# Where the transposed X of a blocked triangular inverse comes from: TensorE's transposes, or VectorE's 32x32 blocks

## The reference, cut to what matters

```python
def wkv_scan(r, decay, k, v, a_vec, b_vec, s0, reverse):
    def step(s, inp):
        r_t, w_t, k_t, v_t, a_t, b_t = inp
        sa = jnp.einsum('bhvk,bhk->bhv', s, a_t)
        s = s * w_t[:, :, None, :] + sa[..., None] * b_t[:, :, None, :] + v_t[..., None] * k_t[:, :, None, :]
        return s, jnp.einsum('bhvk,bhk->bhv', s, r_t)
```

## Time and profile before

| | us |
|---|---|
| median of 3 runs | 3042.59 (3038.54 to 3043.01) |
| profiled execution, own time | 3039.05 |
| profiled execution, span | 3036.8 |
| recurrence, first to last start of `begin_x` (15 steps) | 383.1 |
| PE busy over the whole span | 2760.7 (91%) |
| DVE, ACT, POOL busy over the whole span | 1139.7, 945.8, 177.7 |

### The profile page before, as it was taken

How to read it: one execution, slowest core, us unless ns; L and a number is a source line. 1 busy time by engine, 2 the same in 40 slices (tenths; PEclk the granted TensorE clock), 3 DMA queues, 4 the chain that set the end, 5 groups by cost and what they waited for, 6 DMA issues and landing times.

```text
span 3036.8 us, 57743 instructions
## 1 busy us (share of the span) xinstructions
PE 2760.7 (91%) x25062; PEld 1841.5 (61%) x25062; DVE 1139.7 (38%) x1685; ACT 945.8 (31%) x1575; POOL 177.7 (6%) x231
## 2 busy tenths in 40 slices
PE   8999999999998999999999989899999988866665
PEld 6877777878777878865333332346788774423332
DVE  4545555545455565442000011423545534000001
ACT  4435454434445555432010001103334321100000
POOL 0002000000002000000000000002223210000000
PEclk9999999999999999999999999999999999978778
DMA  6474245575663355534999999711000027999998
GB/s 252 178 284 158 98 142 184 188 276 192 232 226 111 125 193 201 181 119 185 408 421 421 421 421 420 316 68 63 10 16 10 10 76 305 380 421 421 418 421 343
DMA packets 101400, 707.11 MB, mean 233 GB/s; under 512 B 11780, under 2 KB 12548, under 8 KB 18224
## 3 DMA queue, kind: packets, MB, share of 16 engines
q1 hardware_dynamic: 90864, 657.17, 55.1%
q10 hardware_dynamic: 9648, 43.91, 3.7%
q0 software_dynamic: 656, 2.52, 0.2%
HBM read 702.47 MB, written 1.07 MB: 232 GB/s over the span
## 4 chain that ended last, share of the span: by engine, by line
PE 67%; DMA 19%; DVE 6%; ACT 5%; issue 2%; SPq 0%; POOL 0%; ACTq 0%; DVEq 0%; POOLq 0%
DMA weight_ring<-in_stream 19%; PE banks L2040 8%; PE banks L650 7%; PE banks L652 7%; PE banks L651 7%; PE banks L1870 3%; PE banks L2405 3%; PE banks L1017 3%; PE banks L1019 2%; PE banks L1018 2%; PE banks L2451 2%; ACT front L1281 1%; PE banks L1177 1%; PE banks L2826 1%; PE banks L2836 1%
## 5 line engine op out<-in xcount | busy, mean ns | idle before, releaser
L2040 PE MATMUL banks<-weight_ring,scratch 128*32 128x256 f32 (+1 forms) x4304 | 560.1, 500 | 153.4 <-DMA weight_ring<-in_stream 151.8
L2040 PEld LDWEIGHTS banks<-weight_ring,scratch 128*32 128x32 f32 (+1 forms) x4304 | 184.1, 128 | 510.5 <-DMA weight_ring<-in_stream 261.6
L647 DVE TENSOR_TENSOR split_high<-weight_ring,split_high 128x1024 fp32r<-128x1024 f32 x198 | 242.1, 1229 | 258.9 <-ACT split_high L642 258.3
L642 ACT CAST split_high<-weight_ring 128x1024 fp32r<-128x1024 f32 x198 | 206.8, 1052 | 288.9 <-PE banks L652 223.1
L2191 DVE TENSOR_TENSOR scratch<-scratch,banks 128x512 f32<-128x512 f32 (+1 forms) x32 | 17.7, 554 | 573.0 <-PE banks L2040 573.0
L1369 DVE TENSOR_TENSOR split_high<-weight_ring,split_high 128x1024 fp32r<-128x1024 f32 x128 | 161.6, 1273 | 160.4 <-ACT split_high L1266 160.4
L650 PE MATMUL banks<-split_high,features_low 128*128 128x512 f32 x480 | 189.8, 395 | 0.0
L652 PE MATMUL banks<-split_high,features_high 128*128 128x512 f32 x480 | 187.1, 390 | 0.0
L651 PE MATMUL banks<-split_high,features_high 128*128 128x512 f32 x480 | 186.8, 389 | 0.0
L1266 ACT CAST split_high<-weight_ring 128x1024 fp32r<-128x1024 f32 x128 | 133.4, 1049 | 165.3 <-PE banks L1019 159.3
L1017 PE MATMUL banks<-split_high,features_low 128*128 128x512 f32 x392 | 158.6, 405 | 11.2 <-DVE split_high L1369 7.6
(11 more groups left out here) (423 smaller groups left out, 4673.4 us busy)
## 6 DMA issues: line engine op xcount, KB each, us to landing
weight_ring<-in_stream SPq DMA_DIRECT2D x624, 1024.0 KB, 10.7
scratch<-in_kept ACTq DMA_DIRECT2D x20, 1024.0 KB, 10.3
scratch<-in_pair_rows ACTq DMA_DIRECT2D x8, 448.0 KB, 3.6
scratch<-in_kept ACTq DMA_DIRECT2D x6, 512.0 KB, 6.5
scratch<-in_lora ACTq DMA_DIRECT2D x2, 1536.0 KB, 17.8
front<-in_gain_rows ACTq DMA_DIRECT2D x5, 512.0 KB, 3.7
bias<-bias_rows POOLq DMA_DIRECT2D x1, 2304.0 KB, 15.6
scratch<-in_routing ACTq DMA_DIRECT2D x1, 1040.5 KB, 4.9
```

The source lines that it names most:

```text
L642: act.copy(split[i % 4][0], source(i)).then_inc(*self.rounded.up())
L647: dve.tensor_tensor(lo, source(i), hi.bitcast(F32), ALU.subtract).then_inc(*self.rest.up())
L2040: last = pe.matmul(self.psum[q * M:(q + 1) * M, (GATE, UP, DOWN)[part], 0:W], left, w[j][:, q * W:(q + 1) * W], start=(k == 0), stop=(k == ...
```

## The change

The four transposes behind each `z` and ACT's copy into XT go. In their place stands `turn_x(u, n)` on DVE: three instructions that turn X's 32x32 blocks in place, the first for the half of X in which rows need not move (g = 0, 128 partitions), the other two for g = 1, where each half of 64 partitions is written into the other half. Levels 1 to 4 turn all 64 columns (256 elements a partition), level 5 only one side (128 elements). PE's `dx` now waits for `x_turned` in place of `x_saved`. Z and XT are indexed by g = h xor c, and `z` writes the PSUM bank LB + g in place of LB + c. The order of the quarters of the array is the same; the banks they write are not.

```diff
-        Z, XT = (ZX[:, o:o + n].rearrange("p (b c) -> p b c", b=2) for o, n in ((0, U // 2), (U // 2, U)))
+        Z = ZX[:, 0:U // 2].rearrange("p (g c) -> p g c", g=2)
+        XT = ZX[:, U:2 * U].rearrange("p (g t c) -> p g t c", g=2, t=4)
...
@@ z
                 for t in range(4):
-                    for h, c in quads:
-                        out = self.psum[half(h ^ c), LB + c, 32 * t:32 * t + 32].rearrange("p (a j) -> p a j", j=2 ** n)
-                        pe.matmul(out, Lab[d][half(c), h ^ c, t, :], side(X[d][half(c), h ^ c, t, :], n, 1 - d), start=True, stop=True)
-                for t in range(4):
-                    last = pe.transpose(self.psum[:, LB + t // 2, 256 + t % 2 * P:256 + (t % 2 + 1) * P], X_rows[d][:, cols(t)], ident[:, :])
+                    for g, c in quads:
+                        out = self.psum[half(g ^ c), LB + g, 32 * t:32 * t + 32].rearrange("p (a j) -> p a j", j=2 ** n)
+                        last = pe.matmul(out, Lab[d][half(c), g, t, :], side(X[d][half(c), g, t, :], n, 1 - d), start=True, stop=True)
                 last.then_inc(*z_ready.up())
@@ dx
                 pe.wait_ge(z_saved.sem, 5 * u + n)
-                pe.wait_ge(x_saved.sem, 5 * u + n)
+                pe.wait_ge(x_turned.sem, 5 * u + n)
                 for t in range(4):
-                    for h, c in quads:
-                        q = h ^ c
-                        at_ = t % 2 * P + c * HD
-                        last = pe.matmul(self.psum[half(c), LB + q, P + 32 * t:P + 32 * t + 32], XT[half(q), t // 2, at_:at_ + HD],
-                                         Z[half(q), c, 32 * t:32 * t + 32], start=True, stop=True)
+                    for g, c in quads:
+                        last = pe.matmul(self.psum[half(c), LB + g, P + 32 * t:P + 32 * t + 32], XT[half(g ^ c), g, t, :],
+                                         Z[half(g ^ c), g, 32 * t:32 * t + 32], start=True, stop=True)
@@ DVE, new
+            def turn_x(u, n):
+                d = u % 2
+                if n == 1:
+                    dve.wait_ge(x_begun.sem, u + 1)
+                else:
+                    dve.wait_ge(x_placed.sem, 5 * u + n - 1)
+                at_ = slice(32 * d, 32 * d + 32) if n == 5 else slice(0, HD)
+                dve.transpose(XT[:, 0, :, at_], X[d][:, 0, :, at_])
+                dve.transpose(XT[half(1), 1, :, at_], X[d][half(0), 1, :, at_])
+                dve.transpose(XT[half(0), 1, :, at_], X[d][half(1), 1, :, at_]).then_inc(*x_turned.up())
@@ DVE, the order of a step
                     place(l, 1)
+                    turn_x(l, 2)
...
                     place(l, 2)
+                    turn_x(l, 3)
...
                     place(l, 3)
+                    turn_x(l, 4)
...
                     place(l, 4)
+                    turn_x(l, 5)
...
                 if l is not None:
                     place(l, 5)
+                if f is not None:
+                    turn_x(f, 1)
@@ ACT, save_z
-                d = u % 2
                 copy(Z, self.psum[:, LB:LB + 2, 0:P], z_ready, 5 * u + n, z_saved)
-                act.copy(side(XT, n, d), side(self.psum[:, LB:LB + 2, 256:512], n, d)).then_inc(*x_saved.up())
```

More of the change, by code:

```diff
@@ L2679, in rwkv_scan @@
         Lr, Lab = ([groups(x) for x in y] for y in (Lr, Lab))
-        X_rows, X = X, [x.rearrange("p (t g c) -> p g t c", t=4, g=2) for x in X]
+        X = [x.rearrange("p (t g c) -> p g t c", t=4, g=2) for x in X]
         PC = self.small[:, 800:832].rearrange("p (u k) -> p u k", u=4)
@@ L2694, in rwkv_scan @@
         (w_added, a_added, kd_ready, b_ready, kt_ready, bt_ready, at_ready, rt_ready, x_begun, lak_masked, lr_masked,
-         x_placed, ht_saved, state_ready, y_saved, bon_summed, bonus_added) = map(sem, (
+         x_placed, x_turned, ht_saved, state_ready, y_saved, bon_summed, bonus_added) = map(sem, (
              "w_added a_added kd_ready b_ready kt_ready bt_ready at_ready rt_ready x_begun lak_masked lr_masked "
-             "x_placed ht_saved state_ready y_saved bon_summed bonus_added").split())
+             "x_placed x_turned ht_saved state_ready y_saved bon_summed bonus_added").split())
         (w_tanh, a_tanh, pinv_ready, pin_ready, pex_ready, pc_ready, a_saved, b_saved, k_saved, r_saved, lab_saved,
-         lakv_saved, x_saved, z_saved, gw_saved, mt_saved) = map(sem, (
+         lakv_saved, z_saved, gw_saved, mt_saved) = map(sem, (
              "w_tanh a_tanh pinv_ready pin_ready pex_ready pc_ready a_saved b_saved k_saved r_saved lab_saved "
-             "lakv_saved x_saved z_saved gw_saved mt_saved").split())
+             "lakv_saved z_saved gw_saved mt_saved").split())
         (ka_halved, t1_ready, nk_begun, nk_ready, rkr_ready, kk_added, bon_ready, eye_placed, state_spread) = map(sem, (
```

## The result

The changed kernel takes 3078.78 us (3070.02 to 3093.08, 4 runs) against 3041.74 us of the kernel before (now the median of 4 runs): a ratio of 1.0128, 95% interval 1.0106 to 1.0151. It is 37 us slower, where 3043 was forecast and 3069 was the top of the range. Its profiled execution took 3080.2 us, with a span of 3078.0.

What follows compares the result with a forecast made beforehand. Bound: a cycle in which PE's work just covers DVE's latency. Edges -6 us and 12.5 steps at +0.52 us (+6.5) summed to +0.5 us, so 3043 us against the 3042.59 median; range 3022 to 3069.

Steps and rivals of the forecast that it cites:

- The bound: Recurrence step: a cycle where PE's work barely covers DVE's latency; PE as bound was a rival, 2996 us, chance 0.06.
- Where the turns bite: Recurrence step: four of five turns stand ahead of something PE needs within 1 us, delaying step 2, 6 and dx(l,2).
- turn 3 covered: turn_x(l,3) ahead of keys, state(b,0), save_ht: DVE's 1.87 us wait covers it, so 0.58 us of transposes counts.
- the turn's size: DVE's turn instructions: 0.375 us for 256 elements, between overlap and none, and 0.20 us for 128.
- the walk: One recurrence step followed instruction by instruction: mean +0.12 us at 0.33 us a turn instruction, +0.52 at 0.375.
- the clock as a case of its own: Rival in the recurrence: PE's longer waits lower its granted clock, +8 to +10 us, 3052 us; chance 0.09.
- slow-turn case: Rival on DVE: turns do not overlap neighbours or are slower; 3048 to 3069 us, 3057 at 0.50 us; chance 0.20.
- The edges: First and last steps of the loop, without an earlier unit's states or without add_offsets: together -6 us.
- The bank: z and dx writing two diagonal quarters into one PSUM bank: costed at nothing; rival up to +3 us a step, chance 0.03.
- The pipe: DVE: the skill's rule that the next operation waits for an empty pipe, set aside because L3101's neighbour starts after 0.33 us.

Runs made afterwards that it cites:

- e3_noturn: Changed kernel without the turns of levels 2 to 5, turn 1 moved behind state 6, every dx reading its result (inverse wrong): 3000.94 us, ratio 0.9864.
- e5_third: Changed kernel with only the first of a turn's three instructions left at levels 2 to 5, in its old place: 3028.51 us, ratio 0.9956.
- e7_warm: Changed kernel with six idle transposes on PE in its wait ahead of each step's second dx: 3070.65 us, ratio 1.0093.
- e2_fill: Changed kernel with PE's four transposes per level put back behind z, their result unread: 3083.21 us, ratio 1.0141.
- e6_split: As e1_behind, but the first of turn 2's three instructions stays ahead of add_offsets: 3013.98 us, ratio 0.9912.
- e1_behind: Changed kernel with turns 2, 4, 5 and 1 moved on DVE behind add_offsets, state 1, state 3 and state 6: 3017.19 us, ratio 0.9922.

## Why the prediction was wrong

- **The bound.** Right that the 46.7 us of transposes would not come back in this order. But PE was nearer to being the bound than I had it: without turns (e3_noturn) a step gains 2.6 us of the about 3.3 gross, so most of the saving is real once nothing stands ahead of the states. The gross itself was read too small: I took the transposes' 0.58 us and missed the 0.11 by which the `z` ahead of them gets shorter.
- **Where the turns bite.** Right, for each of the four: the waits of PE ahead of `step` 2, 4, 6 and the second `dx`, DVE issuing `add_offsets` right behind a turn, turn 3 covered. Moving them gave the 62 us that the same instructions cost in the wrong place.
- **The step that failed: the turn's size.** I took 0.375 us for an instruction of 256 elements, the middle between overlap and none, and 0.20 us for 128. By itself the first of the three takes 0.37 (e5_third); but the two behind it cross between the halves of the partitions, and neither overlaps what stands ahead of it or behind it. So in the changed kernel the three take 0.45 to 0.47 each, and 0.32 to 0.34 at level 5. Each of the four turns of levels 2 to 5 adds 0.12 us for the wait on the `place` ahead of it, which I left out although the change adds that wait. Turns 2 and 4 are 1.5 us and turn 1 is 1.4, not 1.13; turn 5 is 1.1 and not 0.6. At full clock and without a pause the step is 26.47 us, and 27.09 with L3118 (this one from e7_warm), mean 26.8, against 25.0: +1.8 us, where the walk had +0.52. The four turns are together 1.5 us longer than the sizes I took, and 1.3 us is missing.
- **The second failure: the clock as a case of its own.** In the twelve steps from the third to the last but one the changed kernel lost 31.4 us. The longer step makes 21 of them. The steps below full clock make 14 more: they ran 19 us over the lengths at full clock, those of the kernel before 5. Pauses took back 4: the pauses of PE that end on no engine came to 4.9 us in the recurrence, against 8.8 before. This split rests on one profile of each kernel, and some of the steps below full clock hold a pause too. I gave the clock a rival with 0.09, priced it at 8 to 10 us and excluded it from the slow-turn case, and the range (3069) did not add them. But e7_warm and e2_fill show that PE's own activity moves the clock, so slow turns, which make PE wait longer, bring a clock loss with them.
- **The edges.** I had -6 us, 4.5 of them in the first, second and last of these steps. Those three took 26.43, 26.94 and 24.40 us against 23.44, 24.44 and 22.41, at clocks of 0.74, 0.94 and 1.00: +7.5 us, a miss of 12. With short turns and at full clock (e5_third) the first took 20.6, a gain as forecast. How the first step's loss divides between the turns and the clock is not settled.
- **The bank.** Costed at nothing, and it is nothing for `z` (ratio 0.9998) and, by the rows, for `dx`. The rule of TensorEngine Tiling (Array Packing), Gotcha 1: PSUM Pressure, in the Trainium skill, that different row tiles cannot use one bank at the same time, did not show in the time here.
- **The pipe.** I set aside the rule of VectorE: DVE Perf Modes in the Trainium skill, The DRAIN you can't avoid, since L3101 and its neighbour overlap. That section goes on: "A next op that is not held starts earlier". The rows have both kinds: around the two instructions that cross between the halves nothing overlaps (0.45 us apart at 0.44 long), and behind the first instruction it does (0.37 at 0.45). To set the rule aside for the whole turn was the mistake.

## What to carry to other kernels

Work that moves to an idle engine must be placed behind that engine's short instructions that the busy engine waits for: the same 15 instructions a step were 37 us slower or 23 us faster than the kernel before by their order alone. Price a new instruction by its full length plus the wait it adds, unless a row shows that this kind, on these partitions, overlaps. And when a change makes TensorE wait more, add the clock to the loss and don't treat it as another case.

## What the runs showed of the hardware

- VectorE's 32-bit 32x32-block transposes of 256 elements last 0.44 to 0.45 us and those of 128 elements 0.31, on 64 partitions as on 128, and also when they write the other half of the partitions.
- What follows a transpose that stays on its 128 partitions starts 0.37 us after it (0.24 for 128 elements; e5_third), as other operations of the kernel with 256 elements start 0.33 apart. A transpose from one half into the other starts only when the instruction ahead has ended, and so does what follows it: 0.44 to 0.48 us apart in the turns of 256 elements of every run. In e6_split both kinds stand beside each other:

```profile
2356.93 0.45 DVE L3070 STREAM_TRANSPOSE scratch<-scratch 128x256 f32<-128x256 f32 x1
2357.30 0.66 DVE L3032 TENSOR_TENSOR scratch<-banks,scratch 128x512 f32<-128x512 f32 x1
2357.88 0.68 DVE L3034 TENSOR_TENSOR scratch<-banks,scratch 128x512 f32<-128x512 f32 x1
2358.59 0.44 DVE L3073 STREAM_TRANSPOSE scratch<-scratch 64x256 f32<-64x256 f32 x1
```

  The addition starts before the transpose ahead of it has ended. The crossing transpose starts 0.71 us after an addition of 0.68, with no wait between them; behind the same addition in e1_behind the transpose on 128 partitions starts after 0.60. Whether the crossing or the 64 partitions do it, no run here separates.
- A wait on the instruction just ahead on VectorE costs 0.12 us: 0.52 against 0.40 behind `place`.
- The mean granted clock of the recurrence was 0.92 with PE busy 81% of it, in many short products, and 0.99 with PE busy 93%. Adding idle transposes inside its waits raised the clock to 0.94 and made the kernel faster.
- Two diagonal quarters of the array writing one PSUM bank in turn run at the same rate as into two banks. A product on quarters takes 0.60 us for 32 records ahead of a full-array transpose and 0.49 ahead of another product on quarters.
